# Decay differences taken inside ScalarE's absolute value, and the carried state product replaced by decay rows multiplied into the cross block

## The reference, cut to what matters

```python
    a_cs = jnp.cumsum(ac, axis=-1)
    decay_in = jnp.exp(segsum(ac))            # exp(cs[l] - cs[s]) for s <= l
    cb = jnp.einsum('bclgn,bcsgn->bcgls', cc, bc)
    y_diag = jnp.einsum('bcgls,bgrcls,bcsgrp->bclgrp', cb, decay_in, xc)
    decay_states = jnp.exp(a_cs[..., -1:] - a_cs)
    states = jnp.einsum('bclgn,bgrcl,bclgrp->bcgrpn', bc, decay_states, xc)
    ...
    y_off = jnp.einsum('bclgn,bcgrpn,bgrcl->bclgrp', cc, states_in, jnp.exp(a_cs))
    return (y_diag + y_off).reshape(b, s, h, p)
```

## Time and profile before

| | us |
|---|---|
| median of three runs (lowest, highest) | 1127.55 (1126.48, 1127.94) |
| profiled execution, whole time | 1126.0 |
| profiled execution, span | 1124.2 |
| PE busy | 1103.1 (98%) |
| DVE busy | 942.5 (84%) |
| ACT busy | 705.2 (63%) |
| POOL busy | 182.8 (16%) |

### The profile page before, as it was taken

The page is one execution under the profiler, slowest core; times in us unless marked ns, Lnnn a source line. Parts: engine busy times, 40 slices in busy tenths (PEclk is TensorE's granted clock), DMA queues, the critical chain, the costliest instruction groups (busy, mean ns, idle before and its releaser), DMA issues.

```text
span 1124.2 us, 23363 instructions
## 1 busy us (share of the span) xinstructions
PE 1103.1 (98%) x8802; PEld 1063.1 (95%) x8802; DVE 942.5 (84%) x1675; ACT 705.2 (63%) x1033; POOL 182.8 (16%) x233
## 2 busy tenths in 40 slices
PE   7999999999999999999999999999999999999997
PEld 6999999999998999999999998999988999999987
DVE  5899887788888978877888888789987789988784
ACT  6777885566665457885766654474867357766531
POOL 1000241111112200000011122011324100433310
PEclk9999999999999999999999999999999999999999
DMA  7575447655557865333655569585343754655571
GB/s 273 164 238 189 168 151 256 248 194 182 177 175 274 311 221 185 116 111 138 217 181 181 185 227 317 183 291 188 118 159 128 263 181 157 218 192 185 180 271 39
DMA packets 43711, 220.17 MB, mean 196 GB/s; under 512 B 8063, under 2 KB 12656, under 8 KB 22640
## 3 DMA queue, kind: packets, MB, share of 16 engines
q1 hardware_dynamic: 31552, 185.25, 47.9%
q0 software_dynamic: 9264, 30.94, 7.6%
q10 hardware_dynamic: 2816, 2.90, 0.8%
HBM read 217.97 MB, written 1.11 MB: 195 GB/s over the span
## 4 chain that ended last, share of the span: by engine, by line
PE 80%; DVE 10%; issue 4%; ACT 3%; POOL 1%; DMA 1%; DVEq 0%; ACTq 0%; POOLq 0%
PE ps L892 62%; PE ps L997 8%; PE ps L1001 4%; DVE w_both L571 3%; ACT w_both L557 2%; DVE work L2546 1%; PE ps L1553 1%; DVE work L2351 1%; DMA work<-running_sums 1%; PE ps_idle L1180 0%; POOL actr L877 0%; PE ps_idle L1068 0%; DMA x<-in_x 0%; POOL actr L833 0%; POOL actr L875 0%
## 5 line engine op out<-in xcount | busy, mean ns | idle before, releaser
L892 PE MATMUL ps<-xh,w_both 128*128 128x256 f32 (+1 forms) x3008 | 549.1, 283 | 0.9 <-DVE work L2888 0.3
L892 PEld LDWEIGHTS ps<-xh,w_both 128*128 128x128 f32 x3008 | 466.3, 189 | 3.9 <-issue 1.7
L571 DVE TENSOR_TENSOR w_both<-raw,w_both 128x2048 fp32r<-128x2048 f32 x176 | 397.4, 2258 | 54.0 <-ACT w_both L557 53.3
L892 PE MATMUL ps<-xl,w_both 128*128 128x256 f32 (+1 forms) x1504 | 423.4, 281 | 0.0
L557 ACT ACTIVATE w_both<-raw 128x2048 fp32r<-128x2048 f32 (+1 forms) x178 | 333.4, 1875 | 88.5 <-PE ps L892 36.4
L892 PE MATMUL ps<-actr,w_both 128*128 128x256 f32 (+1 forms) x2460 | 304.5, 283 | 1.0 <-DVE actr L3305 0.8
L892 PEld LDWEIGHTS ps<-actr,w_both 128*128 128x128 f32 x2460 | 295.7, 188 | 7.2 <-issue 4.0
L892 PEld LDWEIGHTS ps<-xl,w_both 128*128 128x128 f32 x1504 | 284.9, 189 | 0.5 <-issue 0.5
L997 PE MATMUL ps<-actr,w_both 128*128 128x512 f32 x396 | 138.1, 393 | 0.0
L818 POOL TENSOR_TENSOR actr<-work,actr 128x256 f32 (+1 forms) x66 | 75.8, 1151 | 356.6 <-ACT actr L1932 356.6
L1001 PE MATMUL ps<-actr,w_both 128*128 128x256 f32 x396 | 108.9, 282 | 0.0
(11 more groups left out here) (310 smaller groups left out, 1077.7 us busy)
## 6 DMA issues: line engine op xcount, KB each, us to landing
raw<-in_up SPq DMA_DIRECT2D x66, 1024.0 KB, 5.0
ada_w<-in_w_ada POOLq DMA_DIRECT2D x54, 256.0 KB, 5.9
raw<-in_xbc SPq DMA_DIRECT2D x12, 1024.0 KB, 5.7
work<-in_w_ada POOLq DMA_DIRECT2D x42, 256.0 KB, 5.8
raw<-in_z SPq DMA_DIRECT2D x8, 1024.0 KB, 4.9
raw<-in_so SPq DMA_DIRECT2D x8, 1024.0 KB, 5.2
raw<-in_dn0a SPq DMA_DIRECT2D x8, 1024.0 KB, 5.2
raw<-in_dn1a SPq DMA_DIRECT2D x8, 1024.0 KB, 6.0
```

The source lines that it names most:

```text
L571: nc.vector.tensor_tensor(wl[:, b % RING, 0:n], raw[:, b % RING, 0:n], wh[:, b % RING, 0:n].bitcast(F32), ALU.subtract).then_inc(lo_done, 1)
L892: mm = nc.tensor.matmul(o, l, r, start=start and n == 0, stop=stop and n == 2)
```

## The change

- `segments` goes. `exps(gr, c)` now waits for the transfer itself, and runs the absolute value as eight instructions of 128x128, one per head, each with the negated running sum of that head as its per-partition bias. The exp stays one instruction of 128x1024.
- `carried`, its bank in the plan, `carried_scaled` and `yoffs` go. ACT takes exp of the running sums of chunk 1 (32 x 128) right after `e12` and writes these rows to memory; POOL's new `chunk_reach(gr)` spreads the 8 rows of a group over 128 partitions (512 KB); DVE's new `crossed(gr)` multiplies them by the cross block (128x1024), where `carried_scaled` stood; `y_by_feature` multiplies `xdte` by that instead of `yoffs` by the identity.
- One of the four running sum matmuls goes, and `e12` is half as wide.
- `chunk_reach(0)` stands between `running_sums(1)` and `(2)`; `chunk_reach(gr + 1)` stands ahead of the `running_sums` that follow `y_by_feature(gr)`.
- `squares_added(1)` moves ahead of `decays(2, 0)`. `x_carried(gr)` waits for `y_by_feature(gr - 1)` instead of `carried(gr - 1)`.

```diff
-            nc.tensor.matmul(ps_dt[:, 224:256], tri[:, 0, :], a_t[:, 1, :], start=True, stop=True)\
...
-            def carried(gr):
...
-                nc.tensor.matmul(bank(g), cbm[:, gr, P:T], xdte, start=True, stop=True).then_inc(misc_done, 1)
...
             def y_by_feature(gr):
...
-                given_back(pe, PL.G[f"yo{gr}"])
+                pe.wait_ge(xdte_done, gr + 1)
+                pe.wait_ge(cross_done, gr + 1)
...
-                            nc.tensor.matmul(o[rows, P:T], yoffs[:, 64 * h:64 * h + 64], ident[:, :],
+                            nc.tensor.matmul(o[rows, P:T], xdte[:, 64 * h:64 * h + 64], reach[:, h, :],
...
             def exps(gr, c):
-                act.wait_ge(seg_done, 2 * gr + c + 1)
+                n = 2 * gr + c
+                act.wait_ge(cs_done, 1)
+                act.wait_ge(csb_in[n % 3], 16 * (n // 3 + 1))
                 d = csb(gr, c).rearrange("p h l -> p (h l)")
-                step.add(A(d, d, ACT.Abs))
+                for h in range(8):
+                    head = csb(gr, c)[:, h, :]
+                    step.add(A(head, head, ACT.Abs, bias=cs_t[:, c, 8 * gr + h:8 * gr + h + 1]))
                 step.wait()
                 A(d, d, ACT.Exp, scale=-1.0).then_inc(seg_exp_done, 1)
...
-            A(e12, ps_dt[:, 192:256], ACT.Exp).then_inc(e12_done, 1)
+            A(e12, ps_dt[:, 192:224], ACT.Exp).then_inc(e12_done, 1)
+            A(reach_rows[32:64, :], ps_dt[32:64, 64:192], ACT.Exp).then_inc(reach_done, 1)
+            act.wait_ge(reach_done, 1)
+            act.dma_start(reach_t.ap(), reach_rows[32:64, :]).then_inc(reach_out, 16)
...
+            def chunk_reach(gr):
+                pool.dma_start(reach.rearrange("p h l -> p (h l)"), reach_of_group(gr)).then_inc(reach_in, 16)
...
             running_sums(1)
+            pool.wait_ge(reach_out, 16)
+            chunk_reach(0)
             running_sums(2)
             for gr in range(3):
                 wait_misc(pool, f"y{gr}", 1)
+                chunk_reach(gr + 1)
...
-            def segments(gr, c):
...
-                V.tensor_tensor(d, d, s, ALU.subtract).then_inc(seg_done, 1)
...
-            def carried_scaled(gr):
...
+            def crossed(gr):
+                dve.wait_ge(reach_in, 16 * (gr + 1))
+                given_back(dve, PL.G[f"cb{gr}"])
+                m = cbm[:, gr, P:T].rearrange("p (a b) -> p a b", a=1).to_broadcast([P, 8, P])
+                V.tensor_tensor(reach, reach, m, ALU.mult).then_inc(cross_done, 1)
...
-            segments(2, 1)
             gated(1, 3)
+            squares_added(1)
             decays(2, 0)
-            squares_added(1)
```

More of the change, by code:

```diff
@@ L157, in make_plan @@
     pl.tile("xbc8", 1)
-    pl.misc("yo0")
     pl.tile("xbc9", 0)
@@ L171, in make_plan @@
     pl.tile("za1", 0)
-    pl.misc("yo1")
     pl.close("gns0")
@@ L181, in make_plan @@
     pl.tile("za2", 1)
-    pl.misc("yo2")
     pl.close("gns1")
@@ L190, in make_plan @@
     pl.close("gns2")
-    pl.misc("yo3")
     pl.tile("za3", 1)
@@ L458, in build_program @@
         csb_in, e12_done = [sem(f"csb_in{b}") for b in range(3)], sem("e12_done")
+        reach_done, reach_out, reach_in, cross_done = sem("reach_done"), sem("reach_out"), sem("reach_in"), sem("cross_done")
         grms_done, skip_done = sem("grms_done"), sem("skip_done")
         pair_squares = sem("pair_squares")
-        seg_done, seg_exp_done = sem("seg_done"), sem("seg_exp_done")
+        seg_exp_done = sem("seg_exp_done")
         ada_in = [sem(f"ada_in{r}") for r in range(4)]
@@ L602, in build_program @@
         xdte = W(6 * KB, 512)
-        yoffs = W(23 * KB, 512)
         zs = W(13 * KB, 4, T)
@@ L606, in build_program @@
         xdt = W(19 * KB, 2, 512)
-        cs_rows = W(12 * KB, P)
+        cs_rows, reach_rows = W(12 * KB, P), W(12 * KB + P, P)
+        reach = ada_w[:, :, :].rearrange("p a n -> p (a n)").rearrange("p (h l) -> p h l", l=P)
         def csb(gr, c):
@@ L678, in build_program @@
         dt_t, a_t = S(2, 32), S(2, 32)
-        e12, ea = S(64), S(32)
+        e12, ea = S(32), S(32)
         lam2, lam4, negl, sgs = S(2), S(2), S(1), S(1)
@@ L705, in build_program, with reach_of_group @@
         sums_t = nc.dram_tensor("running_sums", (64, P), F32, kind="Internal")
+        reach_t = nc.dram_tensor("reach_rows", (32, P), F32, kind="Internal")
+        def reach_of_group(gr):
+            return bass.AP(reach_t, 8 * P * gr, [[0, P], [1, 8 * P]])
         def sums_of_group(gr, c):
@@ L1159, in running_sum_matmuls @@
                 nc.tensor.matmul(ps_dt[0:64, 64:192], a_all, tri[:, 0, :], start=True, stop=True)
-                nc.tensor.matmul(ps_dt[:, 192:224], later[:, :], a_t[:, 0, :], start=True, stop=True)
-                nc.tensor.matmul(ps_dt[:, 224:256], tri[:, 0, :], a_t[:, 1, :], start=True, stop=True)\
+                nc.tensor.matmul(ps_dt[:, 192:224], later[:, :], a_t[:, 0, :], start=True, stop=True)\
                     .then_inc(cs_sums, 1)
@@ L1266, in _ @@
             slab_tile("xbc8", 1)
-            carried(0)
             slab_tile("xbc9", 0)
@@ L1280, in _ @@
             slab_tile("za1", 0)
-            carried(1)
             group_sums(0)
@@ L1290, in _ @@
             slab_tile("za2", 1)
-            carried(2)
             group_sums(1)
@@ L1299, in _ @@
             group_sums(2)
-            carried(3)
             slab_tile("za3", 1)
@@ L1736, in running_sum_copies @@
                 A(cs_rows[0:64, :], ps_dt[0:64, 64:192], ACT.Copy).then_inc(rows_done, 1)
-                A(cs_t.rearrange("p c h -> p (c h)"), ps_dt[:, 256:320], ACT.Copy).then_inc(cs_done, 1)
+                A(cs_t.rearrange("p c h -> p (c h)"), ps_dt[:, 256:320], ACT.Copy, scale=-1.0).then_inc(cs_done, 1)
                 act.wait_ge(rows_done, 1)
@@ L1764, in y_square @@
                     act.wait_ge(rows_out, 16)
+                    act.wait_ge(reach_out, 16)
                 act.wait_ge(gated_done, m + 1)
@@ L2606, in x_carried @@
                 if gr:
-                    wait_misc(dve, f"yo{gr-1}")
+                    wait_misc(dve, f"y{gr-1}", 1)
                 dve.wait_ge(e12_done, 1)
@@ L2680, in _ @@
             masked(3)
-            segments(0, 0)
             split_lo(dve, PL.S["xbc10"])
@@ L2684, in _ @@
             split_lo(dve, PL.S["xbc11"])
-            carried_scaled(0)
+            crossed(0)
             decays(0, 0)
             taps3(9)
-            segments(0, 1)
             split_lo(dve, PL.S["za0"])
-            segments(1, 0)
             decays(0, 1)
@@ L2707, in _ @@
             gated(0, 3)
-            segments(1, 1)
             squares_added(0)
@@ L2711, in _ @@
             group_inverse(0)
-            carried_scaled(1)
+            crossed(1)
             split_lo(dve, PL.S["za2"])
@@ L2718, in _ @@
             y_norm(0, 3)
-            segments(2, 0)
             split_lo(dve, PL.S["zb2"])
@@ L2736, in _ @@
             decays(2, 1)
-            carried_scaled(2)
+            crossed(2)
             split_lo(dve, PL.S["zb3"])
@@ L2754, in _ @@
             squares_added(2)
-            segments(3, 0)
-            segments(3, 1)
             group_inverse(2)
             x_dt(3, 1)
-            carried_scaled(3)
+            crossed(3)
             split_lo(dve, PL.S["so"] + 0)
```

## The result

| | before | after |
|---|---|---|
| median of six runs each, us (lowest, highest) | 1126.53 (1125.45, 1127.94) | 1132.22 (1130.81, 1132.6) |
| profiled execution, whole time, us | 1126.0 | 1132.6 |
| profiled execution, span, us | 1124.2 | 1130.8 |

The ratio is 1.0050 (95% interval 1.0038 to 1.0061): the changed kernel is slower by 5.7 us at the medians, and its profiled execution by 6.6. The forecast was 1131.2, 3.6 above before. Sign and mechanism came out; two terms of the sum were too small.

The account below looks back on a forecast made before the run. PE bound it, elementwise engines only just ahead at 90-100 us. Won 3.4 products, 1.4 stall, 1.6 clock; lost 8.4 in new stalls: 1.9 slower, plus 1.63 clock: 1129.6, plus 1.55 median offset: 1131.2; range 1126.3 to 1134.8.

Parts of the forecast that it names:

- the bias form's size: ACT, each block: eight short biased absolute values take 2.50 us, 1.45 more than before, 11.6 us over eight blocks.
- the lower rival: ACT hides the eight short instructions if they cost below 0.25 us each; kernel not slower, down to 1121; chance 0.10.
- The gap at y0: PE ahead of y_by_feature(0): new stall of 2.4 us waiting for decays, ready at 95.4; block 1.6 us late.
- xt2: Transposes on PE, needing the bank of silu_z(1,1): start at 128.4 instead of 125.74, 2.7 us late, stall 1.3.
- the gap at y3: PE ahead of y_by_feature(3): stall of 1.3 us, second decays ending near 163.5; block 1.9 us late.
- The stall at y1: PE ahead of y_by_feature(1): adds at most half a microsecond, counted as 0.5 us.
- rival 1: ACT hides the short instructions: down to 1121 if all hidden, about 1126 at 0.21 us each; chance 0.10.
- the gap at y2: PE ahead of y_by_feature(2): stall of 2.9 us, start 142.1, as ACT waits for block 5's later transfer.
- rival 4: Extra transfer delays blocks 5 and 7 a full 3.9 us, y_by_feature(2) by 3.2 more than forecast: 1134.4; chance 0.10.
- one fall: PE's clock drops to its lower level once, after the gap at y_by_feature(0) or y_by_feature(2), costing 1.63 us.
- were done a tile or more ahead of PE, which I take to hold: Splits of so, behind ACT's exps: assumed still finished ahead of PE, as before.
- the old gap at the group sums: PE ahead of group 1's sums: the 1.37 us stall and 1.63 us of lower clock behind it go, a gain.

Follow-up runs that it names:

- The first experiment: Kernel before with the bias part alone (eight biased absolute values on ACT, no DVE subtraction, carried products kept): 1127.64 us, 1.0014 against before.
- the last experiment: Changed kernel's bias form and replaced carried products, with decay rows requested behind the first running sums and crossed(2) ahead of decays(2,1): 1127.19 us, 1.0001 against before.
- the replacement alone: Changed kernel with the subtraction back on DVE at its old places and one absolute value per block: 1130.31 us, 1.0037 against before.

## Why the prediction was right, and where it was too small

**Right: the bias form's size, and where it hurts.** A block took 2.44 us, forecast 2.50 from one row of another stage; the lower rival needed less than 0.25 us per instruction and had 0.305. The gap at y0 was 2.39 (forecast 2.4), its start 95.56 (95.4); xt2 was 3.05 late (2.7) on the line named, `silu_z`; the gap at y3 was 1.22 (1.3). The wait at the group sums of group 1 went and ACT inherited the transfer's. The stall at y1 was 1.01 (0.5) and that at xt2 0.83 (1.3), which nearly cancel. The first experiment and the last rule out rival 1. The Trainium skill, page "ScalarE: Activation LUTs", section "What ACT_TABLE_LOAD costs", gave 2.44 us per block as an estimate, and 387 ns and 293 ns for one instruction with and without the pointer; the trace agrees (388 and 297).

**Too small: the gap at y2.** It was forecast at 2.9 and was 3.80, and PE arrived 0.5 later than forecast (139.7 for 139.2). The step that failed is "Request 5 landed at 131.5 ... and now lands at 134.2 ... I take 0.7", which makes 134.9: it landed at 135.84. POOL issued it at 127.03, 2.07 late, and so 0.6 earlier than forecast (2.15 and 0.53), but it took 8.81 us, 2.3 more than before; I had added 0.7, and rival 4 has 3.9. From the landing to y2 another 7.7 us passed, 0.5 more than forecast. The exchange of POOL's requests gave back 2.6 us of gap, and the clock behind it.

**Too small: the clock.** I counted one fall at the old size of 1.63. There was one fall in this stretch, and it cost half as much again, 2.54 us: seven of the 1 us rows have the lower level, four in the kernel before, and it lay on the short matmuls of y2. Filling the gap gave 2.60 at y3. A second fall, near 426 us, cost 0.4, as a wait of 1.1 us in the attention stage, there in the kernel before, covered the rest.

**Wrong: "were done a tile or more ahead of PE, which I take to hold".** The split that the first tile of `so` needs did hold (162.07). What I had left out is its PSUM bank: `silu_z(3, 1)`, behind ACT's exps, started at 170.40 instead of 162.81, and `so` lost 0.47 us.

The account of the profiled executions: forecast 3.5 (without the medians' offset), + 0.9 gap and 0.5 arrival at y2, + 0.9 clock, + 0.5 at `so`, is 6.3 of the 6.6.

**Luck in the number.** The forecast time, 1131.2, is only 1.0 below the median of 1132.22, but the change that it forecast, 3.6, is 2.1 below the 5.7 measured. The two differ because the forecast added 1.55 us for the median of three runs over the profiled execution. Over six runs the median of the kernel before stands 0.5 above that execution, and that of the changed kernel 0.4 below its own. Taken together, the offsets made up for 1.9 of the 3.0 us by which the sum itself, 1129.6, fell short of the profiled 1132.6.

**Missed as an idea, not as a number.** I treated the old gap at the group sums as a gain of the change (1.4 and 1.6). It was to be had without it: moving one subtraction gave 2.3 us. So the change's own worth is less than it seemed: with orders put right, the replacement brings 0.9966 against 0.9980, some 1.6 us of the 3.4 that it takes off PE, and the bias form costs 3.9. With the bias form the replacement brings 1.0001 against 1.0014, some 1.5 us. The two pairs agree, but each difference is no larger than its own uncertainty (1.9 and 1.4 us), so its size stays open.

Open as well: which executions get a fall of the clock and where. The gap at y0 (2.39 us) was followed by none in the changed kernel, but by one in the profile of the exchanged requests (2.42 us, PE's rows at 96 to 99 have 0.50 to 0.71); that at y2 came with one at 3.80 us and with none at 3.56 in the kernel without the bias; and the replacement alone had one behind a gap of 0.57.

## What to carry to other kernels

Cutting one long instruction into eight with a bias each, to save one on another engine, was paid on the engine that got the cut: price it by the distance of short instructions there, and look at the stretch that feeds the bottleneck, not at the share over the span. When an edit adds a transfer, its place in the issuing queue is part of the edit: the same 512 KB cost 4.8 us ahead of an urgent request and next to nothing behind it. Before an existing gap is booked as a gain of a change, try to remove it alone; and a gap that an unrelated wait sets also swallows delays in front of it, so an edit that costs nothing today may cost once that gap is closed (a guess: the cut without the bias was not run on the kernel whose gap is closed).

## What the runs showed of the hardware that was not expected

- A gap of PE can cost more than itself. With one of 3.80 us the granted clock was 0.50 to 0.56 from 142 to 149 us and 24 short matmuls took 5.3 us instead of 2.8. It is not the same in each execution: the kernel before ran in 1124.7 us at a mean clock of 0.998 and in 1129.2 at 0.993, a spread as large as the effect of this change. Differences of single profiles are misleading below that; medians of many runs aren't.
- Three transfers of 512 KB requested one behind the other did not share evenly: each landed behind the one asked for ahead of it. In the changed kernel the three from 98.7 us on landed 4.0, 6.0 and 9.3 us after their issues, those from 126.5 on 7.8, 8.8 and 9.5. A request by itself took 3.9 or 5.7 us in the kernel before. At the place of block 5 the first of three took 6.7 us in the run with the requests exchanged and 8.0 in the last experiment. So what block 5 lost by its place in the changed kernel is the 1.5 us between the first landing (134.3) and its own; why the first took 7.8 is open. (The middle number of the earlier trace rows, 6.9, counts ACT's small write too; the eight reads alone have 7.1, and 8.3 in the changed kernel.) The Trainium skill, page "DMA: Bandwidth & Descriptors", section "Anatomy of one DMA — SWDGE (gpsimd) path", fits 2.0 us plus bytes over 436e3, an estimate of 3.2 us: a lower bound here, not a price, as no such read took less than 3.6.
- A per-partition bias added 91 ns to an instruction of 128x128 on ACT (388 in the changed kernel, 297 in the cut without the bias), and eight in a row took 2.44 us, 0.305 each.
